# Where in SBUF the streamed halves of the activations start

## What is computed

```
proj = u @ in_w            # u: 256 x 1024, in_w: 1024 x several thousand
y.astype(u.dtype) @ out_w
v = rmsnorm(h, g_ffn[i]) @ w_up[i]
h = h + (jax.nn.gelu(v_gate) * v_val) @ w_down[i]
```

## Time and profile before

| | us |
|---|---|
| median of 3 runs | 855.64 |
| the three runs | 855.64, 857.55, 849.83 |
| profiled execution | 856.84 |
| its span | 855.1 |
| TensorE matmul busy | 835.9 (98%) |
| GpSimd busy | 623.2 (73%) |
| VectorE busy | 527.4 (62%) |
| ScalarE busy | 485.5 (57%) |

### The profile page before, as it was taken

How to read it: one execution, slowest core, us unless ns; L and a number is a source line. 1 busy time by engine, 2 the same in 40 slices (tenths; PEclk the granted TensorE clock), 3 DMA queues, 4 the chain that set the end, 5 groups by cost and what they waited for, 6 DMA issues and landing times.

```text
span 855.1 us, 18202 instructions
## 1 busy us (share of the span) xinstructions
PE 835.9 (98%) x7017; PEld 804.2 (94%) x7017; DVE 527.4 (62%) x1543; ACT 485.5 (57%) x925; POOL 623.2 (73%) x282
## 2 busy tenths in 40 slices
PE   8999999999999999999999999999999999999995
PEld 8999988889998899999999989988999999999995
DVE  5997658873244535445458998875666676641164
ACT  6754466664546456563846457875644544554362
POOL 3899855655997455554889899454968888889681
PEclk9999999999999999999999999999999999999998
DMA  8667633332775343434566667433646566667511
GB/s 324 201 215 218 188 121 100 100 99 72 217 221 161 120 137 112 145 101 124 154 217 189 184 203 227 136 88 117 199 142 209 181 189 182 189 190 224 179 50 50
DMA packets 38678, 138.46 MB, mean 162 GB/s; under 512 B 4416, under 2 KB 4544, under 8 KB 38592
## 3 DMA queue, kind: packets, MB, share of 16 engines
q1 hardware_dynamic: 38592, 137.30, 52.4%
HBM read 136.23 MB, written 1.05 MB: 161 GB/s over the span
## 4 chain that ended last, share of the span: by engine, by line
PE 77%; DVE 5%; ACT 2%; issue 1%; POOL 1%; DVEq 0%; ACTq 0%
PE ps L640 21%; PE ps L642 20%; PE ps L641 20%; PE ps L861 1%; DVE ps L1730 1%; POOL wl L583 1%; PE ps L647 1%; PE ps L767 1%; ACT wh L1132 1%; PE ps L649 1%; PE ps L648 1%; PE ps L667 1%; DVE cx L1994 1%; PE ps L885 1%; PE ps L994 1%
## 5 line engine op out<-in xcount | busy, mean ns | idle before, releaser
L583 POOL TENSOR_TENSOR wl<-raw,wh 128x1024 fp32r<-128x1024 f32 x254 | 606.0, 2412 | 192.0 <-ACT wh L1132 191.6
L640 PE MATMUL ps<-uh,wh 128*128 128x256 f32 (+1 forms) x1248 | 353.1, 283 | 1.8 <-POOL wl L583 0.8
L642 PE MATMUL ps<-uh,wl 128*128 128x256 f32 (+1 forms) x1248 | 348.9, 280 | 0.0
L641 PE MATMUL ps<-ul,wh 128*128 128x256 f32 (+1 forms) x1248 | 348.8, 279 | 0.0
L1132 ACT ACTIVATE wh<-raw 128x1024 fp32r<-128x1024 f32 (+1 forms) x255 | 262.8, 1052 | 83.9 <-PE ps L642 76.4
L640 PEld LDWEIGHTS ps<-uh,wh 128*128 128x128 f32 (+1 forms) x1248 | 234.5, 188 | 3.6 <-issue 1.6
L641 PEld LDWEIGHTS ps<-ul,wh 128*128 128x128 f32 (+1 forms) x1248 | 236.4, 189 | 0.0
L642 PEld LDWEIGHTS ps<-uh,wl 128*128 128x128 f32 (+1 forms) x1248 | 233.8, 187 | 0.1
L1823 DVE TENSOR_TENSOR h<-ps,h 128x256 f32<-128x256 f32 x32 | 13.6, 424 | 101.7 <-PE ps L642 101.6
L641 PE MATMUL ps<-ffl,wh 128*128 128x256 f32 x176 | 49.5, 281 | 0.0
L640 PE MATMUL ps<-ffh,wh 128*128 128x256 f32 x176 | 49.5, 281 | 0.0
(11 more groups left out here) (363 smaller groups left out, 1680.2 us busy)
## 6 DMA issues: line engine op xcount, KB each, us to landing
raw<-slabs SPq DMA_DIRECT2D x255, 512.0 KB, 4.1
h<-x_fm SPq DMA_DIRECT2D x4, 256.0 KB, 4.7
out_fm<-outb SPq DMA_DIRECT2D x4, 256.0 KB, 2.2
cst<-shape_consts SPq DMA_DIRECT2D x1, 768.0 KB, 9.4
vec<-vectors SPq DMA_DIRECT2D x1, 299.5 KB, 9.2
pin<-p_fm SPq DMA_DIRECT2D x1, 256.0 KB, 4.8
raw<-slabs SPq DMA_DIRECT2D x1, 128.0 KB, 2.7
vec<-vectors SPq DMA_DIRECT2D x1, 4.0 KB, 2.4
```

What stands on the lines that cost most here:

```text
L583: nc.gpsimd.tensor_tensor(wl[:, s % PART_RING, :], raw[:, s % RAW_RING, :], wh[:, s % PART_RING, :].bitcast(f32), ALU.subtract).then_inc(s ...
L640: nc.tensor.matmul(res, w_h, a_h, start=first, stop=False)
L641: nc.tensor.matmul(res, w_h, a_l, start=False, stop=False)
L642: ins = nc.tensor.matmul(res, w_l, a_h, start=False, stop=last)
```

## The change

`ar` gets an argument `at`, the place modulo 512 B at which a tile of 256 B or more begins; without it the tile begins at 0. Eight pairs of split tiles get one:

| tiles | high part at | low part at |
|---|---|---|
| uh, ul | 0 | 128 |
| ynh, ynl | 256 | 256 |
| ogh, ogl | 384 | 384 |
| cnh, cnl | 128 | 0 |
| onh, onl | 256 | 0 |
| mh, ml | 128 | 128 |
| ffh, ffl | 0 | 256 |
| cqh, cql, ckh, ckl, cxh, cxl, hgh, hgl, ph, pl | 0 | 0 |

The weights stay at 64. The rounding moves the tiles that come behind in the arena up by 512 to 1664 B, each to the same place modulo 512 B as before. The one tile that is not kept there is `dtn` (256 B), which goes from 256 to 0. No instruction, wait, semaphore or transfer is added, removed or put elsewhere.

```
-        def ar(name, shape, dt=f32):
+        def ar(name, shape, dt=f32, at=0):
+
             n = int(np.prod(shape)) * 4
             if n >= PIECE // 2:
-                cursor[0] += -cursor[0] % (PIECE if n >= PIECE else PIECE // 2)
+                cursor[0] += (at - cursor[0]) % PIECE
...
-        uh, ul = ar("uh", [KD, T], f32r), ar("ul", [KD, T], f32r)
+        uh, ul = ar("uh", [KD, T], f32r, 0), ar("ul", [KD, T], f32r, 128)
         after_u = cursor[0]
-        ynh, ynl = ar("ynh", [16, T], f32r), ar("ynl", [16, T], f32r)
+        ynh, ynl = ar("ynh", [16, T], f32r, 256), ar("ynl", [16, T], f32r, 256)
...
-        ogh, ogl = ar("ogh", [16, T], f32r), ar("ogl", [16, T], f32r)
+        ogh, ogl = ar("ogh", [16, T], f32r, 384), ar("ogl", [16, T], f32r, 384)
...
-        cnh, cnl = ar("cnh", [4, T], f32r), ar("cnl", [4, T], f32r)
+        cnh, cnl = ar("cnh", [4, T], f32r, 128), ar("cnl", [4, T], f32r, 0)
...
-        onh, onl = ar("onh", [4, T], f32r), ar("onl", [4, T], f32r)
+        onh, onl = ar("onh", [4, T], f32r, 256), ar("onl", [4, T], f32r, 0)
...
-        mh, ml = ar("mh", [KD, T], f32r), ar("ml", [KD, T], f32r)
+        mh, ml = ar("mh", [KD, T], f32r, 128), ar("ml", [KD, T], f32r, 128)
...
-        ffh, ffl = ar("ffh", [KF, T], f32r), ar("ffl", [KF, T], f32r)
+        ffh, ffl = ar("ffh", [KF, T], f32r, 0), ar("ffl", [KF, T], f32r, 256)
```

## The result

The changed kernel takes 862.21 us (median of 4, 861.82 to 863.82) against 852.74 us for the kernel before (median of 4, 848.97 to 857.55). The ratio is 1.0115 with a 95% interval of 1.006 to 1.017: slower by about 1%, where 843 was forecast.

What follows compares the result with a forecast made beforehand. The prediction took TensorE's matmul count times their distance to bound the kernel: 9.7 us saved in four slow stretches plus 3.9 us credited elsewhere, 13.6 us off 856.84, gave 843.2 us, with a range of 830 to 865.

Steps and rivals of the forecast that it cites:

- What bounds the kernel: Whole kernel: time is nearly the matmul count times their distance, at two levels, 117.8 and 113.4 ns.
- (a): ynh/ynl, onh and ffl at 256: stream meets load 320/512 of the way in, far from the boundary between matmuls.
- (b): ogh/ogl at 384: stream meets load 192/512 of the way in, far from the boundary between matmuls.
- (c): ul, cnh, mh, ml at 128: meeting at 448/512, again near a boundary, so either level is possible.
- (d): uh at 0, low part at 128: two of three boundaries carry a 128 B jump; neither level seen under such jumps.
- the sum: Projection matmuls: 3,400 slow ones of some 5,900 turn fast at 4.4 ns, 13.6 us credited together, giving 843.2 us.
- the meeting of load and stream at an eighth of the way: Stream at 0, load at 64: they meet 64/512 in, where a short delay can move the meeting across the boundary.
- Rival 4: Slower: the jump between uh and ul keeps u slow, and og, on and m lose their place; 868 us, chance 0.16.
- Rival 1: No tie between address and level: the engine's history decides; time as before, 855.6 us with scatter, chance 0.13.
- the sign that I had named for it: If restarts pick levels by chance, unmoved tiles (cql) and moved ones change alike, and runs scatter by some 7 us.
- Rival 3: Below the fast level: offsets put the meeting where nothing is lost, 1.9 ns less for 5,900 matmuls; 832 us, chance 0.13.
- The scatter: Earlier runs span 7.7 us; one was taken to have the 630 to 815 us stretch fast, worth 6.9 us.

Runs made afterwards that it cites:

- micro_1: Program without the model, only TensorE: matmul sections with streams at each multiple of 32 B, weights at 64, four breaks; 38 steps took 4.31 us at place 0, 4.56 at 64.
- all_256: Changed kernel with all 24 split tiles at 256: 856.59 us, ratio 0.9988 to the kernel before.
- u_only: Kernel before with only ul moved to 128: 859.76 us against 854.92, ratio 1.0066.
- micro_5: Program without the model: 18 kinds of break at four layouts, plus 8 and 16 B steps around two; low weights at 192 with streams at 0 gave 113.3 to 113.4 ns.
- all_128: Changed kernel with all 24 split tiles, high and low, at 128: 861.03 us, ratio 1.0081 to the kernel before.
- all_64: Changed kernel with all 24 split tiles at 64, the place of the weights: 874.34 us against 856.42, ratio 1.0234.
- micro_4: The grid: program without the model, 512 layouts of low weights and high and low activations, two breaks each; none under 113.3 ns, two at it after both.
- micro_3: Program without the model: all operands in one tile at written-out places, single operands moved; ten breaks at each of two layouts gave 113.3 or 117.8 ns.

## Why the prediction was wrong

*What bounds the kernel.* Right: the time is the number of matmuls times their distance, and the two levels are 113.3 and 117.8 ns. The 7.0 us between the profiles are all matmul busy time.

*The step that failed: "The change part by part", (a) to (d), and with it the sum.* I let the meeting of load and stream at an eighth of the way be the cause of the slow level, and so took every other place for a way out of it. The grid has it the other way round: the place of before is one of two out of 512 that had the fast level after both breaks, and whether it runs at 113.3 or 117.8 there is settled at the restart, while at the new places of `u`, `og`, `m` and `cn` it is 117.8 nearly always. (a) `yn`, `onh` and `ffl` at 256 changed nothing, as the period is 256 B and not 512 (`micro_1`, `all_256`); I had said that no row showed the 512, and then used it. (b) `og` at 384 and (c) `m` at 128 went from fast to slow (277 to 280, 276 to 280 ns); `cn`, with its high part at 128, lost the fast level too. (d) `u` with its low part at 128 is slow always (`u_only`, 18 of 18 breaks in `micro_5`).

*The sum.* Each of its terms, 3,400 slow matmuls that turn fast, had the wrong sign or was zero. The size of a level change, 4.4 ns, and that it comes onto the path in full, were nearly right: 1,755 matmuls times 4.4 are 7.7 us, and 7.0 were measured.

*Rival 4, slower, is what happened*: `u`, `og` and `m` lost their place, as it says, but not by the jump between `uh` and `ul`, which `all_128` does without. It said 868 against the measured 862.2, as it also charged the matmuls that kept their place modulo 256 B. I gave it 0.16 because "nearly six in ten matmuls are already slow and can't lose"; that holds, and the rest were enough. The rows that could have warned me lay in the three fast stretches: since 0 was able to reach 113.4, within 2 ns of the load's own 111.5, it had more to lose than to gain from a place about which nothing was known. That 862.2 lies within the range of 830 to 865 is no merit of the forecast, which had the sign wrong.

*Rival 1* (no tie) is refuted: `all_64` was put at 874 beforehand and gave 874.3. It was half right, in that at the place of before the level does depend on the restart. By the sign that I had named for it (`cql`, unmoved, changing like the moved groups) it fails too: `cql` went from 278 to 279 ns, `ogl` and `ml` to 280. *Rival 3* (below the fast level) found nothing: no layout of the grid is under 113.3. The rule of the Trainium skill on two independent read ports ("TensorE: Matmul & The Clock Gate", section "Step-by-step: what each phase is for") doesn't hold in this respect: the same loads and streams go from 113.3 to 122 ns apart with their places alone (`micro_4`).

*The scatter* was read rightly: the runs of before fall in two groups 7 us apart, as one long stretch at one level or the other would make them (`all_256`). In the changed kernel `u`, which runs ahead of every such stretch, has one level only, and the runs lie within 2 us. The medians so differ by 9.5 us where the profiles differ by 7.0: two of the four runs of before were of its lower group.

## What to carry to other kernels

Where a weight load and a stream run side by side for the same time (128 float32 columns loaded, 256 streamed), their places against each other modulo 256 B are worth up to 8% of the matmul rate; so measure the distance of starts, not the durations, and compare it with that of the load alone before moving anything. A layout can have more than one level; look for one that has a single level after every kind of break, and try each break in more than one program, since the same break led to different levels here. A program with only TensorE, which tries hundreds of layouts in one execution, says more than a dozen versions of the kernel.

## What I had not expected of the hardware

- The commonest distances, less the columns at 2.4 GHz, are multiples of 2.2 ns: 6.7 (at 113.3), 11.1 (117.8), 13.3 (120.0, and most often at 288 to 384 columns), and 20.0 (place 0 at 512 columns). Others lie between (118.3 and 118.8 at 256 columns; 11.6 to 16.7 over the columns at 288 to 512). No run explains them.
- The high and low weights at 64 and 192, half a period apart, had no slow section after 18 breaks; at 64 and 64 they had one in the same program and eleven in twenty in another (`micro_5`, `micro_3`).
- A shift of the activations by 8 B costs 6.6 to 8.3 ns per matmul (`micro_5`).
- One VectorE instruction took 9.07 us instead of 0.55 while GpSimd ran without a gap, and ended 0.4 us after GpSimd did.
